# Delta rule: four copies and two gate reads move from VectorE to ScalarE

## What is computed

```python
def gated_delta_chunked(q, k, v, g, beta):
    ...
    kb = kc * bc
    m = jnp.where(strict, einsum("nbhid,nbhjd->nbhij", kb, kc) * decay, 0.0)
    t = triangular_solve(eye + m, eye, left_side=True, lower=True, unit_diagonal=True)
    u = t @ (vc * bc)
    w = t @ (kb * jnp.exp(cum_g)[..., None])
    qk = einsum("nbhid,nbhjd->nbhij", qc, kc) * decay
    def step(state, xs):
        v_new = u_i - w_i @ state
        o = (q_i * jnp.exp(g_i)[..., None]) @ state + qk_i @ v_new
        state = (state * jnp.exp(g_last)[..., None]
                 + einsum("bhcd,bhce->bhde", k_i * jnp.exp(g_last - g_i)[..., None], v_new))
        return state, o
# in hybrid_mixer: proj = h @ w_in gives, among others, gz and gate_b
#   yg = rms_norm(o) * gain * silu(gz);  merged = sigmoid(gate_a) * yr + sigmoid(gate_b) * yg
```

## Time and profile before

| | |
|---|---|
| median of 3 runs | 2793.9 us (2793.37 to 2794.67) |
| profiled execution, its own time | 2793.75 us |
| its span, first to last instruction | 2791.9 us |
| TensorE busy | 2748.7 us, 98% |
| VectorE busy | 1946.2 us, 70% |
| ScalarE busy | 1361.9 us, 49% |
| granted TensorE clock, mean | 0.998 |

### The profile page before, as it was taken

The page is one execution under the profiler, slowest core; times in us unless marked ns, Lnnn a source line. Parts: engine busy times, 40 slices in busy tenths (PEclk is TensorE's granted clock), DMA queues, the critical chain, the costliest instruction groups (busy, mean ns, idle before and its releaser), DMA issues.

```text
span 2791.9 us, 38094 instructions
## 1 busy us (share of the span) xinstructions
PE 2748.7 (98%) x15488; PEld 2413.4 (86%) x15488; DVE 1946.2 (70%) x2593; ACT 1361.9 (49%) x1758; POOL 59.4 (2%) x103
## 2 busy tenths in 40 slices
PE   9999999999999999999999999999999999999998
PEld 8899888888888888888888888888888888888887
DVE  7655567778766668999998985467667656666556
ACT  5434654347444446655565644444345434444434
POOL 0000210000000000000000000000000000000000
PEclk9999999999999999999999999999999999999999
DMA  7454444565555544434443455554354555554553
GB/s 273 186 196 159 148 174 184 189 238 194 204 189 204 188 171 165 151 138 149 137 150 136 160 179 204 197 190 157 136 211 182 192 199 196 197 209 182 193 199 151
DMA packets 72847, 506.61 MB, mean 181 GB/s; under 512 B 8385, under 2 KB 8513, under 8 KB 12897
## 3 DMA queue, kind: packets, MB, share of 16 engines
q1 hardware_dynamic: 71136, 497.83, 48.1%
q0 software_dynamic: 1104, 5.90, 0.6%
q10 hardware_dynamic: 432, 0.45, 0.0%
HBM read 499.95 MB, written 2.10 MB: 180 GB/s over the span
## 4 chain that ended last, share of the span: by engine, by line
PE 86%; DVE 10%; ACT 2%; issue 1%; DMA 1%; SPq 0%; POOL 0%; DVEq 0%; ACTq 0%
PE double L1401 80%; PE bank L1401 5%; DVE wlo L2123 2%; DVE cacc L2129 2%; DVE Tn L2637 1%; ACT whi L1775 1%; DVE cst L2146 1%; PE bank L1404 0%; DVE Cm L2123 0%; DVE cst L2123 0%; DVE cacc L2126 0%; DVE gz L2123 0%; DVE AA L2129 0%; ACT TT L2010 0%; DMA vec<-in_vec 0%
## 5 line engine op out<-in xcount | busy, mean ns | idle before, releaser
L1401 PE MATMUL double<-AA,whi 128*128 128x512 f32 (+1 forms) x5008 | 1615.8, 376 | 3.7 <-DVE wlo L2123 3.6
L1775 ACT ACTIVATE whi<-raw 128x1024 fp32r<-128x1024 f32 x926 | 924.8, 1048 | 768.5 <-PE double L1401 712.7
L1401 PE MATMUL double<-AA,wlo 128*128 128x256 f32 (+1 forms) x4624 | 1276.8, 276 | 0.0
L2123 DVE TENSOR_TENSOR wlo<-raw,whi 128x1024 fp32r<-128x1024 f32 (+1 forms) x934 | 1101.0, 1215 | 191.7 <-ACT whi L1775 188.7
L1401 PEld LDWEIGHTS double<-AA,whi 128*128 128x128 f32 x5008 | 917.1, 188 | 171.2 <-DVE wlo L2123 5.2
L1401 PEld LDWEIGHTS double<-AA,wlo 128*128 128x128 f32 x4624 | 867.7, 188 | 1.3
L1401 PE MATMUL double<-whi,AA 128*128 128x512 f32 x1536 | 477.9, 386 | 0.0
L1401 PEld LDWEIGHTS double<-whi,AA 128*128 128x128 f32 x1536 | 288.1, 188 | 51.4 <-DVE wlo L2123 0.2
L1401 PE MATMUL double<-whi,BB 128*128 128x512 f32 x1024 | 309.5, 382 | 0.0
L1401 PE MATMUL double<-wlo,AA 128*128 128x512 f32 x768 | 293.7, 382 | 0.0
L1401 PEld LDWEIGHTS double<-whi,BB 128*128 128x128 f32 x1024 | 191.8, 187 | 33.8
(11 more groups left out here) (340 smaller groups left out, 1738.8 us busy)
## 6 DMA issues: line engine op xcount, KB each, us to landing
raw<-in_wall SPq DMA_DIRECT2D x462, 1024.0 KB, 4.9
raw<-in_wall SPq DMA_DIRECT2D x9, 256.0 KB, 6.4
X<-in_xT SPq DMA_DIRECT2D x1, 2048.0 KB, 11.4
Mm<-in_memT POOLq DMA_DIRECT2D x1, 2048.0 KB, 17.2
tmp<-rqk POOLq DMA_DIRECT2D x16, 128.0 KB, 2.2
mblk<-in_memT SPq DMA_DIRECT2D x8, 256.0 KB, 3.5
dec<-in_dec POOLq DMA_DIRECT2D x1, 1536.0 KB, 10.3
hs<-in_hsT SPq DMA_DIRECT2D x4, 272.0 KB, 5.4
```

The lines of the kernel that those rows point to most:

```text
L1401: return q.matmul(out, lhsT, rhs, start=start, stop=stop, skip_group_check=True)
L1775: q.activation(hi_of(j)[:, c], raw[j % RAW][:, c], ACT.Copy).then_inc(S("w_hi"), 1)
L2123: return q.tensor_tensor(out, a, b, o)
```

## The change

ScalarE takes over: the two halves of Ce (a copy with scale -1), the copy of the last block into TT, both copies of U, and the output of the second tile (the first tile's stays on VectorE). For both gates ScalarE now reads PSUM itself: for gz it makes a copy of each half, scaled by the token factor, and a sigmoid with the same scale; for gtb the sigmoid only. VectorE's step of each gate is gone. The PSUM buffer of a gate is given free by ScalarE's `sig` count rather than VectorE's `ev`. The order of the steps in the list stays. The diff, cut:

```diff
+    def ev_psum_gate(stage, then):
+        def f(tag, h, bs, full):
+            a, b = tmp.take(), tmp.take()
+            tmp.held.update((a[0], b[0]))
+            r = {"t": (a[0], b[0]), "tf": (a[1], b[1]), "b": bs, "full": full, "sig": up("sig", 4 if stage == "gz" else 2)}
+            tasks.append(g_gate(stage, h, r, then))
+            return "sig", r["sig"]
+        return f
...
-    ev_gz_all, ev_gtb_all = ev_token_gate("gz", None), ev_token_gate("gtb", gate_done)
+    ev_gz_all, ev_gtb_all = ev_psum_gate("gz", None), ev_psum_gate("gtb", gate_done)
...
-        r = add("g_up64", h, x=x, b1=b1, f1=f1, p1=up("gdn_pe"), c=up("gdn_vec", 2))
-        side.free(b1, "gdn_vec", r["c"])
+        r = add("g_up64", h, x=x, b1=b1, f1=f1, p1=up("gdn_pe"), c=up("gdn_act", 2))
+        side.free(b1, "gdn_act", r["c"])
...
-        r = add("g_down64", h, c=c, b2=b2, f2=f2, p2=up("gdn_pe"), x=up("gdn_vec"))
+        r = add("g_down64", h, c=c, b2=b2, f2=f2, p2=up("gdn_pe"), x=up("gdn_act"))
...
-            r = add("g_v", (h, t_), b=b1, bf=f1, p=up("gdn_pe"), v=up("gdn_vec"))
+            r = add("g_v", (h, t_), b=b1, bf=f1, p=up("gdn_pe"), v=up("gdn_act"))
...
-            r = add("g_o", (h, t_), b=b2, bf=f2, p=up("gdn_pe"), y=0 if t_ else up("gdn_vec", 2), o=up("gdn_vec"))
+            r = add("g_o", (h, t_), b=b2, bf=f2, p=up("gdn_pe"), y=0 if t_ else up("gdn_vec", 2), o=up("gdn_act" if t_ else "gdn_vec"))
...
 # ScalarE's program
+        def psum_gate(keep):
+            def f(h, r):
+                q.wait_ge(S("w_used"), r["full"])
+                if keep and h:
+                    q.wait_ge(S("gdn_vec"), at["g_end", 2 * h - 1]["v"])
+                d = double[r["b"]][:, :].rearrange("p (m x) -> p m x", m=2)
+                for m in range(2):
+                    if keep:
+                        q.activation(gz[m][:, :], d[:, m, :], ACT.Copy, scale=ftok[:, m:m + 1]).then_inc(S("sig"), 1)
+                for m in range(2):
+                    free(r["tf"][m])
+                    q.activation(tmps[r["t"][m]][:, :], d[:, m, :], ACT.Sigmoid, scale=ftok[:, m:m + 1]).then_inc(S("sig"), 1)
+            return f
...
+        def s_g_up64(h, r):
+            q.wait_ge(S("gdn_pe"), r["p1"])
+            for t, x in enumerate(HALF):
+                q.activation(by_tile(Ce[x, :, :], t), by_tile(bg(r["b1"])[x, :, :], t), ACT.Copy, scale=-1.0).then_inc(S("gdn_act"), 1)
+        def s_g_down64(h, r):
+            q.wait_ge(S("gdn_pe"), r["p2"])
+            q.activation(TT_[h % 2][EARLY, :, LATE], bh(r["b2"])[EARLY, :, :], ACT.Copy).then_inc(S("gdn_act"), 1)
+        def s_g_v(key, r):
+            h, t_ = key
+            q.wait_ge(S("gdn_pe"), r["p"])
+            q.activation(flat(U[:, 2 * t_:2 * t_ + 2, :]), bank[r["b"]][:, 0:256], ACT.Copy).then_inc(S("gdn_act"), 1)
+        def s_g_o(key, r):
+            h, t_ = key
+            if t_:
+                q.wait_ge(S("gdn_pe"), r["p"])
+                q.activation(ob[:, 1, :], bank[r["b"]][:, 0:256], ACT.Copy).then_inc(S("gdn_act"), 1)
...
 # VectorE's program: s_gz, s_g_up64, s_g_down64 and s_g_v are gone, s_g_o keeps tile 0
-            q.tensor_copy(ob[:, t_, :], bank[r["b"]][:, 0:256]).then_inc(S("gdn_vec"), 1)
+                q.tensor_copy(ob[:, 0, :], bank[r["b"]][:, 0:256]).then_inc(S("gdn_vec"), 1)
```

More of the change, by code:

```diff
@@ L298, in evac @@
     def evac(stage, idx, b, full, by="ev", **more):
-        s = 0 if stage in ("u", "k", "v", "gab", "res", "rv", "rg", "gta", "gz", "gtb") else up("sum")
+        s = 0 if stage in ("u", "k", "v", "gab", "res", "rv", "rg", "gta") else up("sum")
         return add(stage, idx, b=b, full=full, sum=s, ev=up(by), **more)
@@ L674, in ev_token_gate @@
         return f
+    def ev_psum_gate(stage, then):
[6 more added lines that the diff above has]
+        return f
     def g_gate(stage, h, r, then):
         ts = r["t"]
-        add(stage + "_sig", h, t=ts, tf=r["tf"], ev=r["ev"], sig=up("sig", 2))
+        if "sig" in r:
+            add(stage + "_sig", h, **r)
+        else:
+            add(stage + "_sig", h, t=ts, tf=r["tf"], ev=r["ev"], sig=up("sig", 2))
         yield
@@ L870, in g_gdn @@
         b2, f2 = side.take()
-        r = add("g_down64", h, c=c, b2=b2, f2=f2, p2=up("gdn_pe"), x=up("gdn_vec"))
-        side.free(b2, "gdn_vec", r["x"])
+        r = add("g_down64", h, c=c, b2=b2, f2=f2, p2=up("gdn_pe"), x=up("gdn_act"))
+        side.free(b2, "gdn_act", r["x"])
         yield
@@ L876, in g_gdn @@
             b1, f1 = side.take()
-            r = add("g_v", (h, t_), b=b1, bf=f1, p=up("gdn_pe"), v=up("gdn_vec"))
-            side.free(b1, "gdn_vec", r["v"])
+            r = add("g_v", (h, t_), b=b1, bf=f1, p=up("gdn_pe"), v=up("gdn_act"))
+            side.free(b1, "gdn_act", r["v"])
             yield
             b2, f2 = side.take()
-            r = add("g_o", (h, t_), b=b2, bf=f2, p=up("gdn_pe"), y=0 if t_ else up("gdn_vec", 2), o=up("gdn_vec"))
-            side.free(b2, "gdn_vec", r["o"])
+            r = add("g_o", (h, t_), b=b2, bf=f2, p=up("gdn_pe"), y=0 if t_ else up("gdn_vec", 2), o=up("gdn_act" if t_ else "gdn_vec"))
+            side.free(b2, "gdn_act" if t_ else "gdn_vec", r["o"])
             if not t_:
@@ L1665, in s_g_down64 @@
             free(r["f2"])
-            q.wait_ge(S("gdn_vec"), r["c"])
+            q.wait_ge(S("gdn_vec"), at["g_down", (h, 32)]["n"])
+            q.wait_ge(S("gdn_act"), r["c"])
             for g in range(2):
@@ L1673, in s_g_v @@
             free(r["bf"])
-            q.wait_ge(S("gdn_act"), at["g_down", (h, 32)]["xd"])
-            q.wait_ge(S("gdn_vec"), at["g_o", (h, 0)]["y"] if t_ else at["g_down64", h]["x"])
+            q.wait_ge(S("gdn_act"), at["g_down64", h]["x"])
+            q.wait_ge(S("gdn_vec"), at["g_o", (h, 0)]["y"] if t_ else at["g_vb", h]["y"])
             for g in range(2):
@@ L1683, in s_g_o @@
             free(r["bf"])
-            q.wait_ge(S("gdn_vec"), at["g_v", key]["v"])
+            q.wait_ge(S("gdn_act"), at["g_v", key]["v"])
             if not t_:
@@ L2010, in s_g_down @@
                 q.activation(odds(TT_[h % 2][x, :, x], d), for_x, ACT.Copy).then_inc(S("gdn_act"), 1)
+        def s_g_up64(h, r):
[14 more added lines that the diff above has]
+                q.activation(ob[:, 1, :], bank[r["b"]][:, 0:256], ACT.Copy).then_inc(S("gdn_act"), 1)
         def s_g_nrm(h, r):
             free(r["tf"])
-            q.wait_ge(S("gdn_vec"), at["g_o", (h, 1)]["o"])
+            q.wait_ge(S("gdn_vec"), at["g_o", (h, 0)]["o"])
+            q.wait_ge(S("gdn_act"), at["g_o", (h, 1)]["o"])
             if h:
@@ L2107, in scalar_program @@
                "gta_sig": token_sigmoid(None), "rtr": s_rtr, "rav": s_rav, "begin_gdn": s_begin_gdn, "cvs": s_cvs, "cvq": s_cvq, "cvn": s_cvn,
-               "gz_sig": token_sigmoid(lambda h, m: gz[m][:, :]), "gtb_sig": token_sigmoid(None), "g_dec": s_g_dec, "g_inv0": s_g_inv0, "g_down": s_g_down,
+               "gz_sig": psum_gate(True), "gtb_sig": psum_gate(False), "g_up64": s_g_up64, "g_down64": s_g_down64, "g_v": s_g_v, "g_o": s_g_o, "g_dec": s_g_dec, "g_inv0": s_g_inv0, "g_down": s_g_down,
                "g_nrm": s_g_nrm, "memn": s_memn, "mv": s_mv, "a4": s_a4, "x_s": s_x_s,
@@ L2600, in s_cvy @@
             stt(x, x, float(128 ** -0.5) if key[1] == 0 else 1.0, tmps[r["t"]][:, :], ALU.mult, ALU.mult).then_inc(S("cnv_vec"), 1)
[L2602 to L2606, removed]
         def s_g_dec(h, r):
@@ L2682, in s_g_vb @@
             tt(four(vb[h % 2][:, :, :]), four(bk(r["b"])), col(beta, h), ALU.mult).then_inc(S("gdn_vec"), 1)
[L2684 to L2698, removed]
         def s_g_o(key, r):
             h, t_ = key
-            q.wait_ge(S("gdn_pe"), r["p"])
             if not t_:
+                q.wait_ge(S("gdn_pe"), r["p"])
                 q.wait_ge(S("gab_vec"), at["gab2", 0]["v"])
@@ L2854, in vector_program @@
                "rsc": s_rsc, "rav": s_rav, "rn": s_rn, "begin_gdn": s_begin_gdn, "conv": s_conv, "cv0": s_cv0,
-               "cv1": s_cv1, "cvv": s_cvv, "cvq": s_cvq, "cvl": s_cvl, "cvy": s_cvy, "gz": s_gz,
-               "gz_in": gate_on(gdn_gate, None, "gz"), "gtb": s_token_gate, "gtb_in": gate_on(gdn_gate, "gz_in", "gtb"), "g_dec": s_g_dec,
-               "g_mat": s_g_mat, "g_inv0": s_g_inv0, "g_up": s_g_up, "g_down": s_g_down, "g_x": s_g_x, "g_up64": s_g_up64, "g_down64": s_g_down64, "g_vb": s_g_vb, "g_v": s_g_v,
+               "cv1": s_cv1, "cvv": s_cvv, "cvq": s_cvq, "cvl": s_cvl, "cvy": s_cvy,
+               "gz_in": gate_on(gdn_gate, None, "gz"), "gtb_in": gate_on(gdn_gate, "gz_in", "gtb"), "g_dec": s_g_dec,
+               "g_mat": s_g_mat, "g_inv0": s_g_inv0, "g_up": s_g_up, "g_down": s_g_down, "g_x": s_g_x,   "g_vb": s_g_vb,
                "g_o": s_g_o, "g_end": s_g_end, "g_tr": s_g_tr, "diag": s_diag, "rmem": s_rmem, "memn": s_memn, "mk": s_mk, "xq": s_xq, "x_s": s_x_s,
```

## The result

The changed kernel takes 2828.7 us (median; 2826.9 to 2835.8) against 2794.3 for the kernel before: a ratio of 1.0125, 95% interval 1.0106 to 1.0145, or 34 us slower. I forecast 2815 and the range 2804 to 2827. The direction was right and the size was not: 34 us where I had 21. The profiled execution took 2826.9 us (span 2825.0), 33.1 us more than that of before. Executions of one kernel differ by some 5 us already before the stage begins (VectorE's first tap of cacc starts between 1057.2 and 1063.8 us in the traces used here), so I also give the span from that tap to the end, called the rest of the span: 1734.0 us in the kernel before, 1767.6 in the changed one.

What follows compares the result with a forecast made beforehand. TensorE was taken to bound the kernel, waiting a little for VectorE in the delta rule. Ce +18.3, gz gates +4.2, gtb +0.4, last gate -1.6 summed to +21.3 us on 2793.9: 2815, range 2804 to 2827 (8 in 10).

Steps and rivals of the forecast that it cites:

- Where the work lies: Delta-rule stage: of 30 us leaving VectorE, only the Ce pair's 0.60 us lies in a first leg; other removals change nothing.
- first leg: Part of a head-pair period from VectorE's restart to Ce, where the VectorE and ScalarE queues set the pace.
- Ce on ScalarE, idle part: Ce queues behind sigmoid and hi pair, so TensorE starts 2.69 us later in six periods, 2.2 in a seventh: +18.3 us.
- the period at 1363.88: Seventh period with the Ce delay; TensorE came late itself, so only 2.2 us was counted.
- My high bound of 3.5 us a period: Upper price of Ce's delay per period, if the queue behind costs something too; seven such entered the range's upper end.
- The gates: ScalarE reading PSUM adds 1.39 us in each of three gz periods (4.2) and 0.12 in three gtb gates (0.4).
- the last gate: Last gtb gate: without VectorE's read, both queues come 1.6 us earlier, shortening TensorE's wait for ob: -1.6 us.
- U: U copies behind a hi pair take about 0.4 us, leaving 0.3 us before TensorE needs them: no cost, but thin.
- Relief: Rival: less VectorE work lets cacc come earlier, so Ce comes on time despite the hi pair; 2786 us, chance 0.07.
- Part of it: Rival: hi pair mostly runs before cacc comes, or a later wait shrinks; +4 to +12, about 2802 us, chance 0.08.
- no difference: Rival: Ce costs nothing more because cvs and hi pair finish in time; gates and ob remain, 2797 us, chance 0.03.

Runs made afterwards that it cites:

- The kernel with the filling products: Changed kernel, with TensorE making 14 products of 512 columns that nobody reads ahead of its wait for Ce in seven periods: 2812.0 us, ratio 1.0058.
- the two kernels without Ce: Changed kernel with Ce back on VectorE: 2797.4 us; kernel before with only TT, U and the second ob on ScalarE: 2794.8 us.
- the best version: Changed kernel with gz back on VectorE and, in ScalarE's queue, Ce, the d = 16 TT pair and the last block's copy moved up: 2781.0 us, ratio 0.9955.

## Why the forecast was wrong in size

**Where the work lies: right.** Only Ce is at the end of the first leg. TT, U and ob on ScalarE changed nothing that can be told (2794.8), and the 24 us less of VectorE work bought no time.

**Ce on ScalarE, idle part: right.** Forecast 2.69 us later, a wait of 3.65 us, +18.3; measured waits of 3.63 to 3.67 and +19.8. The difference is the period at 1363.88, where I granted 2.2 because TensorE came late itself. It had its dip of the clock 10 us earlier in the kernel before; in the changed kernel it had none there, and waited 3.66 us.

**The step that failed** is the one from the wait to the time: "TensorE starts at 1439.52, 2.69 us later" was taken as the whole price of a period, 6 x 2.69 = 16.1 us. After a wait of 3.63 to 3.67 us TensorE also worked at 1.2 GHz for a while: another 14.3 us over seven periods, 2.0 us each on the mean (1.1 to 2.7). The sum put this at nothing without a reason, though the timeline of before held a dip of the same kind. The kernel with the filling products shows the term: 2828.7 down to 2812.0 with Ce arriving no earlier. With that term, and less the dip of before, 21.3 + 14.3 - 1.6 = 34 us, which is the result. It comes out so well by some luck: the idle time of Ce was 1.5 us more than forecast and the rest of the waits 2.0 less. My high bound of 3.5 us a period was made from queue effects and left the clock out, so the range ended 1.7 us short.

**The gates: right in kind, a little high.** 4.6 us forecast less 1.6 at the last gate, 3.0 net; measured 2.7 to 2.9 net between the two kernels without Ce. In the changed kernel the waits show less of it: Cm 2.2 us more, ob 1.3 less. ScalarE in a gz period:

```profile
1415.86 2.01 ACT L1789 ACTIVATE whi<-raw 128x1024 fp32r<-128x1024 f32 x2 [2.54 <-PE double L1414]
1417.78 1.24 ACT L1978 ACTIVATE gz<-double,ftok 128x512 f32<-128x512 f32 x2
1420.33 1.27 ACT L1981 ACTIVATE tmp<-double,ftok 128x512 f32<-128x512 f32 x2
1421.49 0.59 ACT L2039 ACTIVATE TT<-bank 64x128 f32<-64x128 f32 x2
```

The two gz copies took 1.24 us and the two sigmoids 1.27 (I had 1.27 and 1.27), but TT followed the hi pair's start by 5.63 us against 4.54 in the earlier trace rows, 1.09 and not 1.39 more. VectorE idled 3.06 us for this TT, where I had said some 4. The wait for ob at the last gate fell from the 1.7 of the earlier trace rows to 0.4.

**U: right.** Each copy took 0.36 us and TensorE never waited for one.

**The rivals.** Relief did not happen: TT, U and ob off VectorE alone changed nothing that can be told, and VectorE had waited for ScalarE already. Of the 13 to 14 us that the best version gains, 7 to 9 come with no work moved at all. The rest came by order too, but in kernels in which ScalarE makes Ce and the last block of TT, and was not tried without that. "Part of it" and "no difference" fell with the seven waits at their full size.

## What to carry to other kernels

Ask of a piece of work not which engine is less busy but what stands ahead of it in the queue that it joins: 0.6 us of work cost 33 us here, because 2 us of work with time to spare stood in front of it. Price a wait of TensorE at its length and then ask whether its clock is still up behind it: in this stage waits of 1.1 us cost 1.1 with few exceptions, waits of 3.7 us cost 5.7 on the mean. And when a stall is removed, check the next copy in the same queue before promising the gain.

## What the runs showed of the hardware

The granted clock held behind nearly all of TensorE's waits of about 1.1 us; in three of the profiled kernels it fell behind one of them (1.06 to 1.07 us: at 1353.85 in the kernel before, at 1430.48 with TT, U and ob alone on ScalarE, at 1134.28 with Ce ahead of the hi pair). It mostly held behind waits of 1.8 us (it fell after one of six), and fell to 1.2 GHz after all seven of 3.6 to 3.7 us in the changed kernel, but after six of seven with Ce alone on ScalarE. How long it stayed low differed between equal waits: the stretch behind it took 4.57 to 6.12 us in the changed kernel. I had not expected that fourteen products whose results nobody reads would make a kernel 17 us faster.

A wait that the list names after an engine's instruction can belong to the next one in its queue: "cacc_r" ended 0.5 us before the product started, the TT copy 0.1 us before. The names in the product's own row (vb,TT) gave the better lead.
